# Half of six late modulation blocks moved from TensorE to ScalarE and GpSimd, and a reordered opening, in a two-stack transformer kernel

## The reference

```python
def adaln_norm(x, c, g, w_ada, b_ada):
    mod = jax.nn.silu(c) @ w_ada + b_ada
    shift, scale, gate = jnp.split(mod, 3, axis=-1)
    h = rms_norm(x, g) * (1.0 + scale[:, None, :]) + shift[:, None, :]
    return h, gate[:, None, :]
```

## Time and profile before

| | us |
|---|---|
| median of three runs | 1026.5 |
| the profiled execution | 1023.85 |
| its span | 1021.7 |
| PE busy | 975.2 (95%) |
| DVE busy | 641.8 (63%) |
| ACT busy | 462.7 (45%) |
| POOL busy | 152.9 (15%) |
| granted TensorE clock, mean | 0.993 of 2.4 GHz |

### The profile page before, as it was taken

How to read it: one execution, slowest core, us unless ns; L and a number is a source line. 1 busy time by engine, 2 the same in 40 slices (tenths; PEclk the granted TensorE clock), 3 DMA queues, 4 the chain that set the end, 5 groups by cost and what they waited for, 6 DMA issues and landing times.

```text
span 1021.7 us, 15161 instructions
## 1 busy us (share of the span) xinstructions
PE 975.2 (95%) x5730; PEld 817.4 (80%) x5730; DVE 641.8 (63%) x1154; ACT 462.7 (45%) x717; POOL 152.9 (15%) x130
## 2 busy tenths in 40 slices
PE   5999899899999899999999999999999999999996
PEld 2799566677886788887888888879998788888885
DVE  4646565674774765665876666675446587666666
ACT  2253555534454644563444444444437344444442
POOL 3005102201980501050000000000015000000000
PEclk9999999899999999999999999999999999999998
DMA  9973355344555336323356655425523336545541
GB/s 374 371 257 140 115 210 189 147 149 154 191 194 199 123 117 244 124 83 124 125 206 218 212 206 185 185 101 197 198 83 125 124 124 216 195 185 185 185 185 41
DMA packets 23672, 178.42 MB, mean 175 GB/s; under 512 B 3744, under 2 KB 4176, under 8 KB 7112
## 3 DMA queue, kind: packets, MB, share of 16 engines
q1 hardware_dynamic: 19408, 166.70, 43.9%
q0 software_dynamic: 2224, 8.94, 3.1%
q10 hardware_dynamic: 1991, 2.14, 0.6%
HBM read 176.72 MB, written 1.05 MB: 174 GB/s over the span
## 4 chain that ended last, share of the span: by engine, by line
PE 88%; DVE 7%; ACT 2%; issue 1%; DMA 1%; POOL 0%; SPq 0%; DVEq 0%; ACTq 0%; POOLq 0%
PE G L963 14%; PE G L965 14%; PE G L964 14%; PE S L1078 8%; PE T L1078 8%; PE S L1077 3%; PE T L1077 3%; PE T L591 3%; PE T L486 2%; PE G L605 2%; PE G L606 2%; PE G L607 2%; PE G L408 1%; DVE wlo L1934 1%; DMA early<-in_ada_w 1%
## 5 line engine op out<-in xcount | busy, mean ns | idle before, releaser
L2064 DVE TENSOR_TENSOR wlo<-ring,whi 128x2048 fp32r<-128x2048 f32 x88 | 154.4, 1758 | 88.8 <-ACT whi L1662 53.4
L963 PE MATMUL G<-whi,hTh 128*128 128x512 f32 (+3 forms) x560 | 198.3, 354 | 4.5 <-DVE hTl L527 2.8
L964 PE MATMUL G<-wlo,hTh 128*128 128x512 f32 (+3 forms) x544 | 186.4, 343 | 0.0
L965 PE MATMUL G<-whi,hTl 128*128 128x308 f32 (+3 forms) x496 | 167.3, 337 | 0.0
L1934 DVE TENSOR_TENSOR wlo<-ring,whi 128x1024 fp32r<-128x1024 f32 (+3 forms) x76 | 121.0, 1630 | 73.0 <-ACT whi L1529 72.7
L1078 PE MATMUL S<-hT,whi 128*128 128x512 f32 x336 | 122.1, 397 | 0.0
L963 PEld LDWEIGHTS G<-whi,hTh 128*128 128x128 f32 x560 | 105.6, 189 | 19.2 <-DVE hTl L527 5.7
L1078 PE MATMUL T<-hT,whi 128*128 128x512 f32 x336 | 120.6, 394 | 0.0
L1529 ACT CAST whi<-ring 128x1024 fp32r<-128x1024 f32 (+3 forms) x76 | 87.8, 1206 | 59.8 <-PE G L965 34.0
L964 PEld LDWEIGHTS G<-wlo,hTh 128*128 128x128 f32 x544 | 102.7, 189 | 8.9 <-issue 1.5
L965 PEld LDWEIGHTS G<-whi,hTl 128*128 128x128 f32 x496 | 93.3, 188 | 5.6
(11 more groups left out here) (365 smaller groups left out, 1790.6 us busy)
## 6 DMA issues: line engine op xcount, KB each, us to landing
ring<-in_ffn SPq DMA_DIRECT2D x44, 1536.0 KB, 6.3
ring<-in_ada_w SPq DMA_DIRECT2D x16, 1024.0 KB, 6.7
ring<-in_dil_w_in SPq DMA_DIRECT2D x16, 1024.0 KB, 4.7
ring<-in_cd_w_in SPq DMA_DIRECT2D x10, 1232.0 KB, 5.5
ring<-in_nsa_w_in SPq DMA_DIRECT2D x8, 1432.0 KB, 11.2
early<-in_ada_w SPq DMA_DIRECT2D x8, 1024.0 KB, 17.3
ring<-in_ab_w_in SPq DMA_DIRECT2D x4, 1440.0 KB, 5.9
vec<-in_vecs POOLq DMA_DIRECT2D x11, 512.0 KB, 5.3
```

The costliest lines, as they stand in the source:

```text
L963: pe.matmul(out_, act_h, w_h, start=first_, stop=False)
L964: pe.matmul(out_, act_h, w_l, start=False, stop=False)
L965: return pe.matmul(out_, act_l, w_h, start=False, stop=last_)
L2064: TT(wlo[b][:, part], ring[:, b, part], whi[b][:, part].bitcast(F32), ALU.subtract).then_inc(st[what + "_lo"], 1)
```

## The change

Two things are changed.

In the opening, the early blocks 2 and 3 are loaded into the buffers of blocks 0 and 1, and so wait until PE is through with those. The first halves of chunks 0 and 1 are loaded between the early blocks, their second halves behind all of them. ACT and DVE split these chunks by halves in a new order, and PE computes the first half of chunk 1 too in the early part, in place of some products that nothing reads. Chunk 2's load waits for the low part of chunk 0's second half, and the first compressed-attention weight stands behind it on SP's queue, as before.

In the attention rounds, the first half of each of the six late blocks takes another way: it is loaded beside the ring (`near_raw`, two buffers), ACT scales each of its four [128, 512] tiles by silu(c) per partition into `near` (`near_scale`), and GpSimd adds the four tiles onto the block's place (`add_near`). PE keeps the second half. `near_scale` of block c (c = 1 .. 5) stands behind the jobs 2 LATE_AT[c] - 4 to 2 LATE_AT[c] - 1, one tile behind each, and its first tile waits until GpSimd has added block c-1, since `near` is a single buffer. `late_sum` of block c waits for GpSimd's adds of block c.

```diff
-            for i in range(2 * LATE_NSA):
-                fetch_late(i)
+            for c in range(LATE_NSA):
+                if c < 2:
+                    sp.wait_ge(used, split0["nsa_in"] + NSA_C - 1 + c)
+                else:
+                    sp.wait_ge(near_scaled, ADA_K * (c - 1))
+                sp.dma_start(near_raw[c % 2][:], late_src(c, 0).rearrange("p (k w) -> p k w", k=ADA_K)).then_inc(near_landed[c % 2], 16)
+                fetch_late(c, 1)
...
         def late_parts(pe, c, bank):
 
-            for half in range(2):
-                n = late_item[2 * c + half]
+            half0 = 1 if c < LATE_NSA else 0
+            for half in range(half0, 2):
+                n = late_item[late_part(c, half) - 1]
...
         def late_sum(dve, c, bank):
 
-            dve.wait_ge(late["part"], 2 * c + 2)
+            dve.wait_ge(late["part"], late_part(c, 1))
+            if c < LATE_NSA:
+                dve.wait_ge(item_done, c + 1)
             dve.tensor_tensor(late_dst[c], late_dst[c], bank[:], ALU.add).then_inc(late["summed"], 1)
...
+            def add_near(c):
+
+                for k in range(ADA_K):
+                    pool.wait_ge(near_scaled, c * ADA_K + k + 1)
+                    ins = pool.tensor_tensor(late_dst[c], late_dst[c], near[:, k, :], ALU.add)
+                    if k < ADA_K - 1:
+                        tl.done(ins)
+                ins.then_inc(item_done, 1)
+
+            pool.wait_ge(mod0_loaded, 16)
+            pool.wait_ge(mod1_loaded, 16)
+            for c in range(2):
+                add_near(c)
             add_compressed(0)
+            add_near(2)
             add_compressed(1)
+            add_near(3)
             add_branch(0)
             add_compressed(2)
-            for q in range(1, 3):
-                add_branch(q)
+            add_near(4)
+            add_branch(1)
+            add_near(5)
+            add_branch(2)
             add_compressed(3)
...
+            def near_scale(c, k):
+
+                if k == 0:
+                    sc_e.wait_ge(near_landed[c % 2], 16 * (c // 2 + 1))
+                    sc_e.wait_ge(item_done, c)
+                sc_e.activation(near[:, k, :], near_raw[c % 2][:, k, :], ACT.Copy, scale=cb[:, k, 0:1]).then_inc(near_scaled, 1)
+
+            def near_quarters(i):
+
+                for c in range(1, LATE_NSA):
+                    if 0 <= i - 2 * LATE_AT[c] + 4 < ADA_K:
+                        near_scale(c, i - 2 * LATE_AT[c] + 4)
...
             def item_quarters(i):
 
+                near_quarters(i)
                 if i >= 2 * H - 3:
                     high_quarter(i - (2 * H - 3))
 
+            sc_e.wait_ge(used, split0["nsa_in"] + NSA_C)
+            for k in range(ADA_K):
+                near_scale(0, k)
```

The opening, cut to its core:

```diff
             for b, block_of in enumerate(EARLY):
+                if b >= 2:
+                    sp.wait_ge(early["part"], b - 1)
...
-                if b == 1:
-                    fetch(0, a["nsa_w_in"][0], KT * NSA_W)
+                if b == 1 or b == 2:
+                    sp.dma_start(ring[:, b - 1, 0:NSA_HALF], a["nsa_w_in"][b - 1][:, 0:NSA_HALF]).then_inc(w1_early_landed[b - 1], 16)
+            for j in range(2):
+                sp.dma_start(ring[:, j, NSA_HALF:2 * NSA_HALF], a["nsa_w_in"][j][:, NSA_HALF:2 * NSA_HALF]).then_inc(landed[j], 16)
...
-            for n in range(1, NSA_C):
+            for n in range(2, NSA_C):
                 fetch(n, a["nsa_w_in"][n], KT * NSA_W)
...
             scaled(0)
             shifted(1)
-            nsa_low(0)
+            first_low(0, 0)
             for t in range(NT):
                 turn_low(dve, "h0", only=t)
-            scaled(2)
+            scaled(2, lambda: first_low(1, 0))
             shifted(3)
+            first_low(0, 1)
             for t in range(NT):
                 turn_low(dve, "h0", only=2 + t)
-            nsa_low(1)
+            first_low(1, 1)
             nsa_low(2)
             nsa_low(3)
```

More of the change, by code:

```diff
@@ L296, in two_stacks @@
         n_split = n_part = 0
-        for name, count in (("nsa_in", NSA_C), ("w1", 2), ("late", 2 * LATE_NSA), ("nsa_out", OUT_C),
+        for name, count in (("nsa_in", NSA_C), ("w1", 2), ("late", LATE_NSA), ("nsa_out", OUT_C),
                             ("dil_in", 2 * DIL_C), ("late_gate", 2 * (LATE - LATE_NSA)), ("dil_out", OUT_C), ("ab_in", AB_C), ("uq", 1), ("ukv", 1),
@@ L307, in two_stacks, with late_part @@
                     n_part += count * (2 if name in HALVED else 1) - (2 if name in APART else 0)
-        late_item = [first["late"] + i for i in range(2 * LATE_NSA)] + [first["late_gate"] + i for i in range(2 * (LATE - LATE_NSA))]
+        late_item = [first["late"] + c for c in range(LATE_NSA)] + [first["late_gate"] + i for i in range(2 * (LATE - LATE_NSA))]
+        def late_part(c, half):
+            return c + 1 if c < LATE_NSA else LATE_NSA + 2 * (c - LATE_NSA) + half + 1
+        near_raw = [sb("near0", [P, ADA_K, ADA_W], over="wlo0"), sb("near1", [P, ADA_K, ADA_W], over="hTh")]
+        near = sb("near", [P, ADA_K, ADA_W], over="whi0")
         w1_early = [u[:, :, 1792:2816].rearrange("p t (k w) -> p t k w", k=4), tok[:].rearrange("p t (k w) -> p t k w", k=4)]
@@ L407, in late_parts @@
                 for k in range(ADA_K):
-                    ins = pe.matmul(bank[32 * k:32 * k + 32, :], cb[:, half * ADA_K + k, :], w[:, k, :], start=(half == 0), stop=(half == 1))
+                    ins = pe.matmul(bank[32 * k:32 * k + 32, :], cb[:, half * ADA_K + k, :], w[:, k, :], start=(half == half0), stop=(half == 1))
                 ins.then_inc(late["part"], 1)
@@ L1718, in hidden_act, with first_high @@
                 sc_e.copy(hidr[:, v, :], S[v][:, 0:256]).then_inc(nsa_s["hidden_act"], 1)
-            nsa_high(0)
-            turn_act(sc_e, "h0")
-            nsa_high(1)
+            def first_high(c, half):
+                if half == 0:
+                    sc_e.wait_ge(w1_early_landed[c], 16)
+                else:
+                    sc_e.wait_ge(landed[c], 16)
+                at = slice(half * NSA_HALF, (half + 1) * NSA_HALF)
+                sc_e.copy(whi[c][:, at], ring[:, c, at]).then_inc(hi_done, 1)
+            first_high(0, 0)
+            for t in range(NT):
+                turn_act(sc_e, "h0", only=t)
+            first_high(1, 0)
+            first_high(0, 1)
+            for t in range(NT):
+                turn_act(sc_e, "h0", only=2 + t)
+            first_high(1, 1)
             sc_e.dma_start(tab[:, P:], a["tables"][:, P:]).then_inc(tab_loaded, 16)
@@ L2167, in early_sum, with scaled @@
                 TT(part, part, S[b % 2][:], ALU.add).then_inc(early["summed"], 1)
+                if meanwhile is not None:
+                    meanwhile()
                 dve.wait_ge(early["full"], b + 1)
                 return part
-            def scaled(b):
-                part, cols = early_sum(b), slice((b // 2) * ADA_W, (b // 2 + 1) * ADA_W)
-                done(STT(part, G[EARLY_BANK[b]][:], 1.0, gain0[:, cols], ALU.add, ALU.mult), vec_used if b == 2 else None)
+            def scaled(b, meanwhile=None):
+                part, cols = early_sum(b, meanwhile), slice((b // 2) * ADA_W, (b // 2 + 1) * ADA_W)
+                done(STT(part, early_bank[b][:], 1.0, gain0[:, cols], ALU.add, ALU.mult), vec_used if b == 2 else None)
                 for t in range(NT):
```

85 lines of the change are left out of this document (53 added, 32 removed).

## The result

The changed kernel takes 1052.43 us (median of 4 runs, 1050.16 to 1054.30); beside it the kernel before took 1025.51 us (4 runs). The ratio is 1.0263, 95% interval 1.0243 to 1.0282: 26.9 us slower. Forecast were 1043 us and 1031 to 1050, so the sign was right and the size was 9.4 us short, outside the range. The profiled span is 1048.4 us against 1021.7 (+26.7), the mean granted clock 0.977 against 0.993.

What follows compares the result with a forecast made beforehand. The prediction took PE, busy 95% of the span, as the bound, with DVE's compressed softmax in the chain in rounds 2 to 5. Its terms, -1.9 + 13.3 + 0.9 + 2.5 + 2.5 = +17.3 us, gave 1043 us, range 1031 to 1050.

Steps and rivals of the forecast that it cites:

- Part 1: Attention rounds: PE's removed halves save 0.96 us each in blocks 0 and 5, -1.9 us.
- Part 2: Late rounds of blocks 2 to 4: late_sum waits for GpSimd adds queued behind a late compressed add, +13.3 us.
- Part 3: Attention rounds: ACT's scaled tiles delay the out rounds and short round 5, +0.9 us, bounds 0 and +3.
- Part 5: Opening: chunk 2's later load brings no gain and chunk 3 comes late, +2.5 us, bounds -3.7 and +5.
- Part 4: Three attention stalls: PE resumes at half clock for some 3 us, 0 to +5 us, taken as +2.5.
- rival (b): Late rounds: GpSimd's adds end before late_sum would run, so PE's halves count; 1019 to 1025 us; chance 0.09.
- Rival (c): Attention stalls: GpSimd's adds slowed to 1.9 us or more each, +7 to +11 us more, 1052 us; chance 0.06.

Runs made afterwards that it cites:

- E5: The whole change plus five unneeded 512-column products on PE in each of rounds 7, 9 and 11 while late_sum waits: 1044.15 us, 1.0187 of the kernel before.
- E3: The whole change with near blocks moved one place earlier in GpSimd's list, ahead of the compressed adds: 1.0035 of the kernel before.
- E6: The changed opening alone, with 20 unneeded 128-column products on PE ahead of chunk 2: 1.0028 of the kernel before.
- E4: Old opening, near halves of all six blocks, GpSimd's list reordered as in E3: 0.9993 of the kernel before.
- E8: Old opening, near halves for blocks 2 to 5 only, no tiles ahead of the attention or in rounds 3 and 5: 0.9984 of the kernel before.
- E7: The changed opening alone, with a compressed weight moved behind chunk 3's load and ACT's tables behind its cast of chunk 2: 1.0018 of the kernel before.
- E10: The changed opening alone, with the table behind the small loads and two compressed weights behind chunks 4 and 5: 0.9988 of the kernel before.
- E11: The loads of E10 together with the four near halves of E8: 0.9988 of the kernel before.
- E12: E11 plus unneeded PE products, eight ahead of chunk 2 and two in round 1: 1.0025 of the kernel before.
- E2: The near halves alone, with the old opening: 1.0215 of the kernel before.
- E1: The changed opening alone, late blocks computed wholly by PE as before: 1.0033 of the kernel before.

## Why the forecast had the sign and missed the size

| step | forecast | measured | from |
|---|---|---|---|
| Part 1, shorter parts, blocks 0 and 5 | -1.9 | -1.7 at full clock and with VectorE not held (5.86 - 6.72, 5.12 - 5.98) | E5, E3 |
| Part 2, late_sum behind GpSimd | +13.3 | +13.1 (10.31 + 10.30 + 10.39 - 3 x 5.98) | E5 |
| Part 3, ACT's tiles | +0.9 | +1.0 (0.9 in round 6, 0.03 each in 8, 10, 12) | after, E5 |
| not in the sum: VectorE held by GpSimd's adds | 0 | +2.0 (0.6, 0.8 and 0.65 in rounds 1, 4 and 13) | after |
| Part 5, the opening's loads | +2.5 | +2.9 | E6 |
| Part 4, the clock | +2.5 | +6.9 behind the stalls, +0.9 in round 2, 1.1 to 1.6 in the opening | E5, E6 |
| sum | +17.3 | about +26.5 | |

**Part 2** held in each detail: the order of the list, the late compressed add, adds 1.34 us apart, PE idle about 5 us. E3 shows that the order is the cause. That is why the chances were right to leave little for rival (b), which asked that the adds be out of the way; E4 and E8 are that case, with medians of 1023.3 and 1023.5 us.

**Part 4 is the step that failed.** It said "some 3 us, which costs about half of that. Over three stalls that is 0 to +5 us; I take +2.5". The runs showed 6.9 us behind the three stalls, and 2 to 2.5 us where no stall had been priced. Three things were wrong. The low stretch is 4 to 5 us of PE's work, not 3, and the trace of before shows nearly 4, had I read on from the earlier trace rows until the clock was back:

```profile
191.00:192.00 1.00, 1.00 (x7) 1.00 (x6) 0.65 (x1) 0.73 (x2) 0.00 (x0) 0.50 0.09 16
192.00:193.00 1.00, 1.00 (x10) 1.00 (x9) 0.00 (x0) 1.00 (x3) 0.00 (x0) 0.92 0.24 33
```

Half of 4 to 5 us is 2 to 2.5 us a stall, and the differences of after and E5 in rounds 7 to 12 sum to 6.9 us. The middle of the bounds was taken where the sentence's own numbers, half of 3 us three times, made 4.5. And the clock was charged to the three stalls only: the shorter parts of block 0 ran at half clock (1.94 us in round 2, what the whole block took before), and so did about half of chunk 2 of the projection.

**Part 3** held. ACT's tiles in the short round 5 delay round 6 by 0.9 us (0.5 forecast) and the other out rounds by next to nothing (0.1 forecast for each). Round 3's tiles are covered by DVE's chain, as told: PE waits 1.09 us for probT in round 4, and then 0.89 us for DVE all the same. So are the four tiles ahead of the attention: PE waits 0.66 us for ACT's probabilities in round 1, and then 2.07 us for DVE.

**What the sum had at nothing** is VectorE's side of GpSimd's adds. The prediction looked for a price of their meeting on GpSimd alone and found its adds undisturbed. The runs show 2.0 us on VectorE, in rounds 1, 4 and 13 (last section).

**Part 5** had the size, but partly by luck. It let chunk 2 start at 51.5 us at no loss and chunk 3 come 2.7 us late. At full clock (E6) the whole loss is ahead of chunk 2, which starts at 54.56 us, 2.8 later than the 51.8 of before; PE doesn't wait for chunk 3 in the changed kernel or in E6.

**Rival (c)** named 1052 us, the number that was measured. That is luck: its mechanism, adds of 1.9 us or more in the stalls, did not happen; they took 1.26 to 1.28 us.

**The range** was too narrow since it let the clock's upper bound be 5 us. With the 9 us and more that were measured in its place the same sum gives about 1050, and VectorE's 2.0 us make nearly all of the rest.

## What to carry to other kernels

An engine that is idle most of the time can still be late, because it works its list in order: look up what stands ahead of the new work in that list and when its input comes, and put the new work ahead of it. A stall of the matrix engine costs its length and then the half-rate work behind it; here 13.1 us of stalls brought 6.9 us more in the rounds beside them, so price every forecast stall twice, from a stretch of the trace that goes on until the clock is back. A load that is issued later must be priced with all that is issued beside it, and moving it forward can make another one late (E7, but not E10). Work given to GpSimd is paid for on VectorE too, where an operation on the critical path falls into one of its adds: place the two apart in time (not tried here), or count the rest of the add for each meeting.

## What had not been expected

**VectorE held by GpSimd's adds.** DVE's small multiply of two SBUF operands takes 0.17 us; when it falls into a near add, it ends only with that add. In round 9 of E3 (DVE's timeline) it takes 0.79 us and ends at 160.03, as does GpSimd's first add of the pair that begins at 158.75 (1.28 us long):

```profile
159.24 0.79 DVE L2392 TENSOR_TENSOR rden<-rden,gate 128x4 f32<-128x4 f32 x1
160.07 0.42 DVE L2395 TENSOR_TENSOR tok<-G,rden 128x256 f32<-128x256 f32 x1
160.53 0.69 DVE L2385 TENSOR_TENSOR tmp<-G,gate 128x512 f32<-128x512 f32 x1
```

The gating behind it (0.69 us) comes late by as much, and PE's parts wait 0.32 us for it. The late rounds of E3 take longer by just what the first such multiply in them takes longer:

| round of E3 | 7 | 11 | 9 | 13 |
|---|---|---|---|---|
| the multiply, us | 0.17 | 0.45 | 0.79 | 0.84 |
| the round, us | 5.12 | 5.40 | 5.75 | 5.79 |

E4, E8, E11 and E12 show the same pairs within 0.02 us, and round 13 of the changed kernel and of E5 fits too (0.82 and 5.78, 0.42 and 5.37). So a late round from 7 on that does not stall takes 4.95 us and the multiply, and a near half is worth 0.86 us only where no add meets it.

Rounds 1 and 4 of the changed kernel lose their time in the same way, and not by ACT's tiles. These are the operations of DVE on the chain there, first before and then after, and the GpSimd adds that the second three fall into (TENSOR_SCALAR reads one tensor, TENSOR_TENSOR two; all of them lie in SBUF):

```profile
116.97 0.21 DVE L2250 TENSOR_SCALAR gate<-gate 128x96 f32<-128x96 f32 x1
131.10 0.66 DVE L2281 TENSOR_TENSOR kT<-kT,tab 128x480 f32<-128x480 f32 x1
132.48 0.18 DVE L2283 TENSOR_SCALAR scm<-scm 128x32 f32<-128x32 f32 x1
```

```profile
121.00 0.83 DVE L2343 TENSOR_SCALAR gate<-gate 128x96 f32<-128x96 f32 x1
135.81 1.15 DVE L2374 TENSOR_TENSOR kT<-kT,tab 128x480 f32<-128x480 f32 x1
137.69 0.45 DVE L2376 TENSOR_SCALAR scm<-scm 128x32 f32<-128x32 f32 x1
```

```profile
120.49 1.27 POOL L920 TENSOR_TENSOR mod<-mod,near 128x512 f32<-128x512 f32 x1
135.17 1.28 POOL L920 TENSOR_TENSOR mod<-mod,near 128x512 f32<-128x512 f32 x1 [2.82 <-ACT near L1850]
136.53 1.57 POOL L920 TENSOR_TENSOR mod<-mod,near 128x512 f32<-128x512 f32 x1
```

The first is longer by 0.62 us, and round 1 by 0.62; the other two are longer by 0.49 and 0.27 us, and round 4 by 0.76. The first takes 0.82 or 0.83 us in all five kernels whose GpSimd adds block 0 there (after, E2 to E5) and 0.21 in the nine others. GpSimd paid once: its add of 1.57 us began while the middle operation was under way.

Operations with a PSUM operand keep their 0.42 and 0.69 us. The Trainium skill ("SBUF — State Buffer", Who interferes with whom) says that a VectorE instruction with two SBUF inputs contends with a GpSimd one that reads SBUF; by its summary the second to issue waits until the first is done. For the multiply the trace agrees, with these numbers. Rival (c) had looked for this price on GpSimd's side, and nearly all of it is on VectorE's.

**The clock near the edge.** With the same instructions, round 2 took 5.86 us (E4, E5), 6.79 and 6.80 (after, E3) and 7.58 (E2) in the profiled executions with a near half for block 0, and 6.72 (before, E1, E7), 7.19 (E6), 7.49 (E8), 8.35 and 8.41 (E10, E11) in those without, by whether and when the clock fell around PE's waits of 2.1 or 1.7 us and less in round 1; the kernel before has the same waits as E8 and E11 and showed 1.00. A gain of one microsecond beside such a place can't be read from one profile.
